# Prompt attention: the second key head's probabilities are scaled inside their transposition

## Chip, cores, metric

One Trainium2 chip, one core of it. The metric is the device time of one execution in microseconds, the median of several runs.

## What is computed

One inference step of a hybrid decoder layer for a prompt of 512 tokens and eight sample groups of four tokens, followed by a mixture of 32 experts. The change lies in the attention of the prompt. There, eight query heads share two key heads (four query heads each). Each query head has three branches, and each branch's result is weighted by a gate that was computed before:

```python
pr = masked_softmax(s + bias, mask)                       # per branch: exp(s - max) / sum
o_slc = einsum("bcgpkl,bcgkld->bcgpd", pr, kv[..., 1, :]) # selected blocks
o_win = einsum("bngpck,bnkgd->bncgpd", pr, kv[..., 1])    # sliding window
o_nsa = gn[0] * o_cmp + gn[1] * o_slc + gn[2] * o_win     # gates, one per token and head
```

With 512 tokens every causal block is selected and the window holds every earlier token, so both branches are causal attention over up to 512 keys.

## The kernel before

The program is a sequence of phases on all engines. Between two phases stands `phase_over()`, which clears the phase's semaphores and holds all engines at a barrier (line 214). The prompt attention is one phase; behind it come the branch gates with the output projection and the routing, and then the experts, which take more than half of the time.

The prompt attention works in **groups**, listed in `GROUPS_P` (lines 1521 to 1523): four groups for the cross-attention into memory (MEMB), one for each tile of 128 tokens, then for the tiles t = 3, 2, 1, 0 one group each of compressed (CMP), selected (SLC) and window (WIN) attention. A group of SLC or WIN has four **query steps**, one for each p in 0 to 3, and each step holds two query heads, one of either key head g; other groups have one step. That makes 40 query steps, 32 of them of SLC and WIN. Turning and multiplying with the values goes by **value steps**: t + 1 for a group of SLC or WIN (one for every 128 keys), one for the others, 28 in all, 20 of them of SLC and WIN.

Time is divided into **slots** (lines 1528 to 1532): slot s holds query step s. The value steps of a group begin three slots after its last query step (`LAG = 3`), one to a slot. Each engine runs its own list of this work in that order, and semaphores join them.

A query step of SLC or WIN, w = 128 (t + 1) keys wide, goes through the engines so:

- TensorE, `queries` (line 1764): one product of 64 x 128 by 64 x w for each g, into its own PSUM bank.
- VectorE, `scores_of` (line 1698): adds the position bias, writes to `probs` in SBUF and takes the maximum, one operation for each g.
- ScalarE, `exponentials` (line 1640): the exponential in place, with the sum of the row.
- VectorE, `scales` (lines 1720, 1721): reciprocal of the two sums, times the gates, into `scale_of`; this comes in VectorE's list between the next step's two scores, and waits until GpSimd is done with the step two before. The product with the gate raises `a_rc`.
- GpSimd (lines 1591 to 1595): waits for `a_rc`, multiplies the w columns of both heads by their factor in place, and raises `a_pr`.

A value step goes so:

- TensorE, `turn` (lines 1767 to 1784): waits until GpSimd has scaled the whole group, then transposes four heads of 128 x 128 for g = 0 into bank 4, and four for g = 1 into bank 5. Each half waits for the copy of the turn before out of its bank.
- ScalarE copies bank 4 (line 1599 through 1608) and VectorE bank 5 (line 1662) to `probT_p`.
- TensorE, `values` (line 1809): one slot later, two products of 128 x 64 by 128 x 512, accumulated over a tile's three branches in one bank.

TensorE's list for a slot is: turn, queries, and the values of the turn of the slot before. VectorE's is: copy of the turn, scores of g = 0, factors of the step before, scores of g = 1. `probs` has three buffers (`RING = 3`), used by groups in turn. A product in float32 shows as two records on TensorE, a transposition as one; each record has a weight load of its own.

SyncE loads the bias tables, the tokens and the first gate weights at the beginning of the phase (lines 1568 to 1576). Neither that nor any other transfer is touched.

Of the kernel before, what the change touches and what calls it, by code (L numbers as in the profile page):

```python
# [18 lines left out]
ALU = mybir.AluOpType  # L19
# [180 lines left out]
def build_program(nc, i, o, stop_after=99):  # L200

    ctx = ExitStack()
    with ctx:
        of_phase = []

        def sem(name):
            of_phase.append(nc.alloc_semaphore(name=name))
            return of_phase[-1]
# [33 lines left out]
        def bank(b, n=1):  # L242
            return psum[:, b] if n == 1 else psum[:, b:b + n]


        ident = take(128)
# [132 lines left out]
        src = lambda n: x[0:rows_of(n), n, :] if n < NT else mem[:, n - NT, :]  # L379
# [1126 lines left out]
        RING = 3  # L1506
        bias_q = take(8, NP_TOK)
        probs = take(RING, 8, 512)
        probT_p = take(2, 2, 512)
        peak = take(2, 8)  # L1510
        total = take(2, 8)
        scale_of = take(2, 8)
        assert cursor[0] <= w_gb_at
        cursor[0] = w_gb_at
        w_gb = take(6, KD, 128)
# [4 lines left out]
        SLC, WIN, CMP, MEMB = range(4)  # L1520
        GROUPS_P = [(MEMB, t) for t in range(TILES)]
# [34 lines left out]
        a_ex = sem("a_ex")  # L1556
        a_rc = sem("a_rc")
        a_pr = sem("a_pr")
        a_tp = sem("a_tp")
        a_ta, a_td = sem("a_ta"), sem("a_td")  # L1560
        a_pv = sem("a_pv")
# [3 lines left out]
        with nc.Block() as block:  # L1565
# [12 lines left out]
            @block.gpsimd  # L1578
            def _(pool):
                for i_q, (n, p) in enumerate(q_steps):  # L1580
                    kind, t = GROUPS_P[n]
                    c = scale_of[:, i_q % 2]
                    pool.wait_ge(a_rc, i_q + 1)
                    if kind == MEMB:
                        pool.tensor_tensor(mem_probs(n), mem_probs(n), c[:, 0:4].unsqueeze(2).to_broadcast([128, 4, MEM]),
                                           ALU.mult).then_inc(a_pr, 1)
                    elif kind == CMP:
                        pool.tensor_tensor(compact(n), compact(n), c.rearrange("q (g p) -> q g p", g=2).unsqueeze(3)
                                           .to_broadcast([128, 2, 4, NCMP_P]), ALU.mult).then_inc(a_pr, 1)
                    else:  # L1590
                        w = 128 * (t + 1)
                        for g in range(2):
                            rows = probs[:, n % RING, 4 * g + p, 0:w]
                            ins = pool.tensor_scalar(rows, rows, c[:, g:g + 1], None, ALU.mult)  # L1594
                        ins.then_inc(a_pr, 1)

            @block.scalar
            def _(act):
# [53 lines left out]
            def _(dve):  # L1652
# [49 lines left out]
                def scales(i_q):  # L1702

                    n, p = q_steps[i_q]
                    kind, t = GROUPS_P[n]
                    tot, c = total[:, i_q % 2], scale_of[:, i_q % 2]
                    gate = gates[:, t].rearrange("q (p g n) -> q n g p", p=4, g=2)
                    dve.wait_ge(a_ex, 2 * i_q + 2)
                    if i_q >= 2:
                        dve.wait_ge(a_pr, i_q - 1)  # L1710
                    if kind == MEMB:
                        dve.reciprocal(c[:, 0:4], tot[:, 0:4]).then_inc(a_rc, 1)
                    elif kind == CMP:
                        link(dve.tensor_reduce(tot.rearrange("q (g p) -> q g p", g=2), compact(n), AX, ALU.add))
                        link(dve.tensor_scalar(tot, tot, 1e-30, None, ALU.max))
                        link(dve.reciprocal(tot, tot))
                        dve.tensor_tensor(c.rearrange("q (g p) -> q g p", g=2), tot.rearrange("q (g p) -> q g p", g=2),
                                          gate[:, 0], ALU.mult).then_inc(a_rc, 1)
                    else:
                        link(dve.reciprocal(tot[:, 0:2], tot[:, 0:2]))  # L1720
                        dve.tensor_tensor(c[:, 0:2], tot[:, 0:2], gate[:, 1 + kind, :, p], ALU.mult).then_inc(a_rc, 1)  # L1721

                for slot in range(SLOTS_P):
                    if (j := turn_at(slot)) is not None:
# [9 lines left out]
            def _(pe):  # L1734
# [32 lines left out]
                def turn(j):  # L1767

                    n, a = v_steps[j]
                    kind, t = GROUPS_P[n]  # L1770
                    pe.wait_ge(a_pr, q_last[n] + 1)
                    for g in range(2):
                        if j:
                            pe.wait_ge((a_ta, a_td)[g], j)
                        for k in range(4):
                            if kind == MEMB:
                                src = mem_probs(n)[:, 2 * g + k // 2, 128 * (k % 2):128 * (k % 2) + 128]
                            elif kind == CMP:
                                src = compact(n)[:, g, k]
                            else:  # L1780
                                src = probs[:, n % RING, 4 * g + k, 128 * a:128 * a + 128]
                            rows = NCMP_P if kind == CMP else 128
                            mm = pe.transpose(bank(4 + g)[0:rows, 128 * k:128 * k + 128], src, ident)
                        mm.then_inc(a_tp, 1)

                def values(j):
# [729 lines left out]
```

## Time and profile before

| | |
|---|---|
| median of 3 runs | 2143.67 us (2143.18 to 2145.86) |
| the profiled execution | 2147.72 us |
| its span, first to last instruction | 2145.8 us |
| its mean granted TensorE clock | 0.946 |
| TensorE busy over the span | 1979.5 us, 92% |
| VectorE | 516.7 us, 24% |
| ScalarE | 407.5 us, 19% |
| GpSimd | 335.2 us, 16% |
| prompt attention | from about 527 to 645 us |

The busy time is a sum over phases with different limits. A group of instructions is named by its line in the kernel; a helper's line stands for all that call it. "Idle before" is the time the engine stood still directly before these instructions, with the engine and line that ended most of it. PE is TensorE's matrix work, PEld its weight loads, which run beside it; DVE is VectorE, ACT ScalarE, POOL GpSimd. PEclk is the granted share of TensorE's 2.4 GHz.

### The profile page before, as it was taken

The page shows a single profiled execution, that of the slowest core. Times are in us where ns is not written, and L with a number is a line of the kernel's source. Part 1 is how long each engine was busy: PE and PEld are TensorE (multiplying, and loading weights), DVE is VectorE, ACT ScalarE, POOL GpSimd, SP SyncE. Part 2 cuts the span into 40 slices and gives each one's busy share as a digit, 9 for nine tenths or more (in the row PEclk, how much of TensorE's full clock was granted, in tenths as well). Part 3 has the DMA queues.
Part 4 walks back from the last instruction along what each step waited for, and adds up shares of the span by engine and source line. Part 5 has one row for each costly group of instructions (what it writes and reads, how often), then busy time and mean ns, then how long its engine had stood idle before and what let it go on. Part 6 is the DMA issues. An engine that isn't in the chain of part 4 may idle for free.

```text
span 2145.8 us, 42699 instructions
## 1 busy us (share of the span) xinstructions
PE 1979.5 (92%) x17225; PEld 1038.0 (48%) x17225; DVE 516.7 (24%) x1342; ACT 407.5 (19%) x960; POOL 335.2 (16%) x359
## 2 busy tenths in 40 slices
PE   7997887788888999995999999999999999999995
PEld 3446773535447888644334444343443434444342
DVE  2224454241650111115211212112121211212111
ACT  3133561011650000000111111111111111111110
POOL 0010000000760000320112121121211112121121
PEclk9997987887999999996899999999999999999997
DMA  8116414231205110001999999999999999999994
GB/s 299 63 49 246 156 51 196 98 138 49 92 1 207 50 59 30 15 30 39 413 390 396 395 395 396 390 397 394 395 396 395 392 391 394 398 394 397 391 398 143
DMA packets 104369, 532.05 MB, mean 248 GB/s; under 512 B 15480, under 2 KB 32640, under 8 KB 52577
## 3 DMA queue, kind: packets, MB, share of 16 engines
q1 hardware_dynamic: 83721, 469.42, 55.4%
q0 software_dynamic: 19824, 59.12, 9.6%
q10 hardware_dynamic: 768, 2.75, 0.3%
q8 instruction: 36, 0.59, 0.1%
q14 instruction: 20, 0.16, 0.0%
HBM read 508.82 MB, written 28.91 MB: 251 GB/s over the span
## 4 chain that ended last, share of the span: by engine, by line
PE 49%; DMA 2%; ACT 1%; issue 0%; DVE 0%; POOL 0%; POOLq 0%; DVEq 0%
PE psum L2425 29%; PE psum L2438 16%; PE psum L2411 1%; PE psum L2474 1%; PE psum L2419 1%; DMA arena<-scr_h,arena 1%; PE psum L2464 1%; DMA y_sum<-arena 1%; ACT arena L2349 1%; POOL y_sum L2320 0%; ACT arena L2354 0%; DVE arena L2376 0%; PE psum L2455 0%; DVE arena L2372 0%; ACT arena L2335 0%
## 5 line engine op out<-in xcount | busy, mean ns | idle before, releaser
L2425 PE MATMUL psum<-arena 128*32 128x512 f32 x6144 | 666.9, 591 | 0.0
L2425 PEld LDWEIGHTS psum<-arena 128*32 128x32 f32 x6144 | 200.9, 108 | 447.3 <-issue 441.5
L2438 PE MATMUL psum<-arena 128*32 128x256 f32 x6144 | 344.8, 379 | 8.2 <-ACT arena L2349 8.2
L2438 PEld LDWEIGHTS psum<-arena 128*32 128x32 f32 x6144 | 191.3, 109 | 143.8 <-ACT arena L2349 15.7
L2390 DVE TENSOR_SCALAR arena<-psum 128x256 f32<-128x256 f32 x96 | 40.8, 425 | 883.0 <-PE psum L2425 880.3
L2320 POOL DMA_INDIRECT y_sum<-arena x96 | 149.3, 1555 | 620.1 <-ACT arena L2354 614.1
L2114 PE MATMUL psum<-arena 128*128 128x272 f32 x768 | 181.8, 394 | 1.4 <-PEq L217 1.4
L2114 PEld LDWEIGHTS psum<-arena 128*128 128x128 f32 x768 | 146.2, 191 | 34.8 <-issue 3.1
L2346 ACT ACTIVATE arena<-arena 128x256 f32<-128x256 f32 x96 | 40.1, 418 | 607.2 <-DVE arena L2390 607.2
L738 PE MATMUL psum<-arena 128*128 128x512 f32 (+3 forms) x320 | 112.5, 510 | 0.2 <-DVE arena L610 0.2
L2354 ACT ACTIVATE arena<-psum,arena 128x256 f32<-128x256 f32 x96 | 45.2, 471 | 187.4 <-PE psum L2438 187.4
L738 PEld LDWEIGHTS psum<-arena 128*128 128x128 f32 (+1 forms) x320 | 50.1, 175 | 62.9 <-issue 62.6
L949 DVE COPY arena<-psum 64x256 f32<-64x256 f32 (+1 forms) x144 | 57.6, 400 | 65.0 <-PE psum L1042 61.1
L2134 PE MATMUL psum<-arena 128*128 128x512 f32 (+1 forms) x160 | 71.1, 604 | 2.2 <-DVE arena L1975 2.2
L1594 POOL TENSOR_SCALAR arena<-arena 128x512 f32<-128x512 f32 (+3 forms) x64 | 68.4, 1082 | 23.8 <-DVE arena L1721 23.7
L1971 DVE TENSOR_TENSOR arena<-psum,arena 128x544 f32<-128x544 f32 x24 | 17.4, 724 | 218.8 <-ACT arena L1949 218.8
L1051 PE MATMUL psum<-arena 128*128 128x256 f32 (+1 forms) x288 | 68.0, 399 | 0.0
L2121 PE MATMUL psum<-arena 128*128 128x272 f32 x256 | 64.2, 399 | 4.1 <-DMA arena<-in_w_up 4.1
L1051 PEld LDWEIGHTS psum<-arena 128*128 128x128 f32 x288 | 57.2, 216 | 8.8 <-ACT arena L960 1.9
L2300 POOL COPY arena<-arena 96x1 uint32 (+1 forms) x33 | 6.1, 184 | 354.1 <-DMA y_sum<-arena 245.7
L1042 PE MATMUL psum<-arena 128*128 128x128 f32 (+1 forms) x288 | 43.1, 316 | 16.8 <-DVE arena L949 15.9
L1949 ACT ACTIVATE arena<-psum 128x544 f32<-128x544 f32 x24 | 15.0, 624 | 227.1 <-PE psum L2121 227.1
(353 smaller groups left out, 1755.2 us busy)
## 6 DMA issues: line engine op xcount, KB each, us to landing
arena<-in_w_gu SPq DMA_DIRECT2D x256, 1024.0 KB, 20.1
arena<-in_w_down SPq DMA_DIRECT2D x128, 1024.0 KB, 16.9
arena<-in_w_gb SPq DMA_DIRECT2D x24, 512.0 KB, 3.5
arena<-in_w_tok SPq DMA_DIRECT2D x3, 2048.0 KB, 10.3
arena<-in_x_all SPq DMA_DIRECT2D x8, 512.0 KB, 5.9
arena<-in_cache_mem SPq DMA_DIRECT2D x8, 512.0 KB, 3.6
arena<-in_cache_win SPq DMA_DIRECT2D x8, 512.0 KB, 4.1
arena<-in_w_up SPq DMA_DIRECT2D x1, 4096.0 KB, 13.4
```

Of the source, the lines that this page charges most:

```text
L738: mm = pe.matmul(bank(2 + c)[0:r, 0:b - a], dstT(n)[:, k], w_tok[:, k, a:b], start=(k == 0), stop=(k == KD - 1))
L949: copy(kvT[64 * a:64 * a + 64, c, 2 * q:2 * q + 2, g, 0:n], b[64 * g:64 * g + 64, :, a]).then_inc(s_kv, 1)
L1042: mm = pe.transpose(bank(q)[:, t * n:(t + 1) * n], rows[:, 4 * q + t, c], ident[0:n, 0:n])
L1051: mm = pe.matmul(bank(4 + c)[:, 0:2 * n].rearrange("p (g n) -> p g n", g=2), w_cmp[:, c, j], kvT[:, c, j, :, 0:n], start=(j == 0), stop=(j ...
L1594: ins = pool.tensor_scalar(rows, rows, c[:, g:g + 1], None, ALU.mult)
L2114: pe.matmul(bank(4 * s + h)[:, 0:HALF], w_gb[:, u % 6, k], hT[:, k, t], start=(k == 0), stop=(k == KD - 1))
L2121: mm = pe.matmul(bank(4 * s + 2 + h)[:, 0:HALF], w_up[:, k, 128 * c:128 * c + 128], oT_of(k)[:, t], start=(k == k0), stop=(k == k1 - 1))
L2134: mm = pe.matmul(bank(2 * (n % 2) + h)[0:r], mixT[:, k, 128 * n:128 * n + r], w_out[:, k, 512 * h:512 * h + 512], start=(k == 0), stop=(k ...
L2320: pool.indirect_dma_start(y_quarters, bass.IndirectOffsetOnAxis(cur_row[:, g:g + 1], 0), y_rows[:, g], None, compute_op=ALU.add).then_inc( ...
L2354: act.activation(y_rows[:, g], dn_half(g), ACT.Copy, scale=cur_gate[:, g:g + 1]).then_inc(e_yc, 1)
L2425: mm = pe.matmul(gu_bank(g)[32 * j:32 * j + 32].rearrange("p (h n) -> p h n", h=2), xgT[:, k, 32 * g:32 * g + 32], w_in_e[:, k, :, 256 * j ...
L2438: mm = pe.matmul(dn_half(g)[32 * j:32 * j + 32], actT[:, g, k % 2, 32 * (k // 2):32 * (k // 2) + 32], w_down_e[:, k, 256 * j:256 * j + 256 ...
```

## The change

The second key head's probabilities are no longer scaled on GpSimd. VectorE writes a 128 x 128 diagonal matrix with the factor (gate over sum) of the second head of each step, and the transposition of these probabilities becomes a float32 product with that diagonal, which turns and scales at once. The diagonals have a ring of three by four buffers beside `probs`. VectorE waits for the factor that it just made before it uses it; a turn of SLC or WIN waits for the diagonals of the group besides GpSimd's scaling. MEMB and CMP groups stay as they were.

```diff
@@ -1510,6 +1510,7 @@
         scale_of = take(2, 8)
+        diag = take(RING, 4, 128)
@@ -1556,6 +1557,7 @@
+        a_dg = sem("a_dg")
@@ -1589,10 +1591,8 @@
                         w = 128 * (t + 1)
-                        for g in range(2):
-                            rows = probs[:, n % RING, 4 * g + p, 0:w]
-                            ins = pool.tensor_scalar(rows, rows, c[:, g:g + 1], None, ALU.mult)
-                        ins.then_inc(a_pr, 1)
+                        rows = probs[:, n % RING, p, 0:w]
+                        pool.tensor_scalar(rows, rows, c[:, 0:1], None, ALU.mult).then_inc(a_pr, 1)
@@ -1719,6 +1719,8 @@
                         link(dve.reciprocal(tot[:, 0:2], tot[:, 0:2]))
                         dve.tensor_tensor(c[:, 0:2], tot[:, 0:2], gate[:, 1 + kind, :, p], ALU.mult).then_inc(a_rc, 1)
+                        dve.wait_ge(a_rc, i_q + 1)
+                        dve.tensor_scalar(diag[:, n % RING, p], ident, c[:, 1:2], None, ALU.mult).then_inc(a_dg, 1)
@@ -1769,6 +1771,8 @@
                     pe.wait_ge(a_pr, q_last[n] + 1)
+                    if kind in (SLC, WIN):
+                        pe.wait_ge(a_dg, sum(1 for m, p in q_steps[:q_last[n] + 1] if GROUPS_P[m][0] in (SLC, WIN)))
@@ -1780,7 +1784,11 @@
                             rows = NCMP_P if kind == CMP else 128
-                            mm = pe.transpose(bank(4 + g)[0:rows, 128 * k:128 * k + 128], src, ident)
+                            out = bank(4 + g)[0:rows, 128 * k:128 * k + 128]
+                            if g and kind in (SLC, WIN):
+                                mm = pe.matmul(out, src, diag[:, n % RING, k], start=True, stop=True)
+                            else:
+                                mm = pe.transpose(out, src, ident)
                         mm.then_inc(a_tp, 1)
```

## Rows read from the trace of the kernel before

**Rows 1.** Busy time by stage; columns: stretch, its length, each engine busy, clock, DMA

```profile
527.00:645.00 118.00, 98.06 (x608) 53.68 (x608) 72.78 (x264) 67.57 (x200) 78.29 (x72) 0.90 0.18 64
645.00:1015.00 370.00, 337.32 (x1378) 247.88 (x1378) 69.34 (x163) 27.14 (x46) 29.89 (x14) 0.93 0.18 59
```

**Rows 2.** Waits, 532 to 648 us: total, times, longest

```profile
PE psum L1783 <- POOL arena L1594: 15.2, 7, 5.3
```

**Rows 3.** Groups by shape, GpSimd, same stretch: busy, mean ns, idle before

```profile
L1594 POOL TENSOR_SCALAR arena<-arena 128x512 f32<-128x512 f32 x16 | 24.7, 1559 | 3.7 <-DVE arena L1721 3.7
...
L1594 POOL TENSOR_SCALAR arena<-arena 128x384 f32<-128x384 f32 x16 | 19.7, 1244 | 6.6 <-DVE arena L1721 6.6
...
L1594 POOL TENSOR_SCALAR arena<-arena 128x256 f32<-128x256 f32 x16 | 14.5, 923 | 5.9 <-DVE arena L1721 5.9
...
L1594 POOL TENSOR_SCALAR arena<-arena 128x128 f32<-128x128 f32 x16 | 9.5, 603 | 7.5 <-DVE arena L1721 7.5
```

**Rows 4.** Timeline, TensorE, 553 to 576 us: start, length, what, idle before

```profile
553.39 2.27 PE L1764 MATMUL psum<-arena 64*128 64x512 f32 x8
560.94 1.97 PE L1783 MATMUL psum<-arena 128*128 128x128 f32 x8 [5.28 <-POOL arena L1594]
...
575.23 1.09 PE L1783 MATMUL psum<-arena 128*128 128x128 f32 x8 [1.43 <-POOL arena L1594]
```

**Rows 5.** Timeline, TensorE, 578 to 645 us

```profile
578.11 1.09 PE L1783 MATMUL psum<-arena 128*128 128x128 f32 x8
579.13 0.92 PE L1764 MATMUL psum<-arena 64*128 64x384 f32 x4
579.98 1.08 PE L1809 MATMUL psum<-arena 128*64 128x512 f32 x4
...
602.14 1.09 PE L1783 MATMUL psum<-arena 128*128 128x128 f32 x8 [2.04 <-POOL arena L1594]
...
623.12 1.97 PE L1783 MATMUL psum<-arena 128*128 128x128 f32 x8 [2.62 <-POOL arena L1594]
...
634.64 1.09 PE L1783 MATMUL psum<-arena 128*128 128x128 f32 x8 [0.65 <-POOL arena L1594]
...
640.63 1.09 PE L1783 MATMUL psum<-arena 128*128 128x128 f32 x8 [2.94 <-POOL arena L1594]
```

**Rows 6.** Busy time and clock of short stretches; columns as in rows 1

```profile
561.00:564.00 3.00, 3.00 (x12) 2.02 (x12) 0.69 (x1) 0.60 (x1) 2.97 (x2) 0.50 0.00 0
...
600.00:602.00 2.00, 0.10 (x2) 0.00 (x0) 1.19 (x6) 1.18 (x4) 2.00 (x2) 1.00 0.00 0
...
623.00:629.00 6.00, 5.88 (x26) 4.45 (x28) 2.56 (x12) 2.56 (x9) 1.81 (x4) 0.50 0.00 0
```

**Rows 7.** Timeline, GpSimd, 545 to 578 us

```profile
548.53 15.44 POOL L1594 TENSOR_SCALAR arena<-arena 128x512 f32<-128x512 f32 x10 [1.83 <-DVE arena L1721]
565.79 9.38 POOL L1594 TENSOR_SCALAR arena<-arena 128x512 f32<-128x512 f32 x6 [1.83 <-DVE arena L1721]
```

**Rows 8.** Timeline, VectorE, 553 to 575 us

```profile
555.57 0.16 DVE L1721 TENSOR_TENSOR arena<-arena 128x2 f32<-128x2 f32 x1
...
557.91 0.17 DVE L1720 RECIPROCAL arena<-arena 128x2 f32<-128x2 f32 x1 [0.92 <-POOL arena L1594]
558.11 0.38 DVE L1721 TENSOR_TENSOR arena<-arena 128x2 f32<-128x2 f32 x1
...
571.29 0.42 DVE L1689 TENSOR_TENSOR arena<-arena 128x248 f32<-128x248 f32 x1
...
573.88 0.44 DVE L1715 TENSOR_SCALAR arena<-arena 128x8 f32<-128x8 f32 x1
```

**Rows 9.** Timeline, TensorE, 230 and 337 us: float32 products on the full array

```profile
230.08 2.75 PE L1051 MATMUL psum<-arena 128*128 128x256 f32 x12
...
337.67 0.38 PE L1366 MATMUL psum<-arena 128*128 128x127 f32 x2
337.88 0.31 PE L1367 MATMUL psum<-arena 128*128 128x32 f32 x2
```

**Rows 10.** Groups by shape, VectorE, whole span

```profile
L2084 DVE TENSOR_SCALAR arena<-arena 128x220 f32<-128x220 f32 x4 | 1.3, 330 | 0.0
```

## The prediction

> **What bounds the kernel now.** I read the views from the outside in. First the engine table by stage: the prompt attention runs from about 527 to 645 us, and the gate and routing stage behind it starts when the last engine of this one has finished [rows 1]. Between the two stands a barrier over all engines, and the only loads for later are issued at its start, so a microsecond won or lost in these 118 us is one in the end time. In the stage TensorE is busy 98.1 us and GpSimd 78.3 us. Neither share says who waits, so next comes the list of waits of the stretch: TensorE's matmuls in the turns (line 1783) stood still 15.2 us behind GpSimd's scaling (line 1594) [rows 2]. That is the most this change can take away directly. Third come GpSimd's four widths: 1.56, 1.24, 0.92 and 0.60 us for 512, 384, 256 and 128 columns, 16 of each, two per step [rows 3].
>
> Then the timeline of TensorE, to see where the 15.2 us lie. They are 5.28 us before 560.94, 1.43 before 575.23 [rows 4], 2.04 before 602.14, 2.62 before 623.12, 0.65 before 634.64 and 2.94 before 640.63 [rows 5]; what is left of the 15.2 is one short wait of 0.2. Between them, from 576 to 598 us and in most of the rest, TensorE is itself the bound: a turn takes 1.02 us to the start of the queries, those 0.85, the value products follow, and nothing stands still [rows 5]. So the change helps TensorE in a few gaps and makes it longer in the stretches between them.
>
> **Removed: 32 scalings on GpSimd**, one of each step's two. Their busy time is half of 68.4 us, or 34.2 us [rows 3], but only what a gap waits for comes back.
> - Gap at 560.94. GpSimd worked without a break from 548.53, ten operations of 1.54 us [rows 6]; the eighth, the end of the fourth step, releases the turn. VectorE had this step's factor ready at 555.57 [rows 7]. With one operation a step GpSimd has no queue there: 555.7 + 0.1 + 1.56 = 557.4. Gain 3.55 us.
> - Gap at 575.23: 1.43 us. One operation less (1.56) covers all of it. Gain 1.43.
> - Gaps at 602.14, 623.12, 634.64, 640.63. In each, GpSimd starts the last step's pair as soon as the factor is there, so one operation of that width goes: 1.24, 0.92, 0.60, 0.60 [rows 3]. The short wait of 0.2 goes too.
> Together 8.5 us. What is late next in these gaps is the chain scores, exponentials, factor; it remains.
>
> **Added on TensorE: 80 products in place of 80 transposes** (20 turns of the selected and window groups, four heads of the second key head). A transpose is one record, and eight come in a turn of 1.09 us, the last lasting 0.27: 0.117 us from start to start [rows 5]. The trace of before has no 128-column product on a full array in this stage. The nearest is line 1366, 127 columns: two records, and the next product starts 0.21 us later [rows 8]. Above it stands line 1051, 256 columns, 12 records in 2.75 us, 0.215 each, or 0.43 us a product [rows 8]. Below, a product could cost no more than the transpose; I see no reason for a gain. I take the nearest, 0.21: about 0.10 us more for each, 80 x 0.10 = 8.0 us, all of it where TensorE is the bound or right behind a gap. Ends: 0 and 80 x 0.32 = 25.6 us.
> The Trainium skill's page TensorE: Matmul & The Clock Gate (Terms, the entry on xbus) says that the transpose mode is four times as fast for FP32. By that rule each product would cost 0.47 us and the sum 28 us; the row of line 1366 says twice, not four times, and the measurement decides.
>
> **Added on VectorE: 32 diagonals**, each behind a wait for the factor made just before. A tensor_scalar of 220 columns takes 0.33 us [rows 9], the factor itself, 2 columns, 0.16 [rows 7]; between them by columns a 128-column one takes 0.26. The wait adds the space between two dependent operations. The reciprocal before a factor shows it: 557.91 to 558.11, 0.20 for an operation of 0.17 [rows 7]. Scores that used to start 0.11 after the factor (555.57) start about 0.3 us later. Queued behind the diagonal are the step's second scores, then ScalarE's exponential. In full slots this is covered: VectorE has some 2.4 us of work (two scores of 0.69, factor pair 0.33, copy 0.69) in a slot of 2.9 to 3.1. The cover is missing in the gaps, where the chain is what TensorE waits for. I count two diagonals before 557, one each before the gaps at 602, 623 and 634, three before the last: 8 x 0.3 = 2.4 us lost. Ends: 0 and, under GpSimd's hand, much more (a rival, below).
> The **new wait of a turn** on the diagonals costs nothing: the diagonal of a step is ready about 0.5 us after the factor starts, and GpSimd, released by the same factor, takes 0.60 at least plus the release. If that cover were gone, it would be 0.1 us for each of eight groups. The copy of the second bank on VectorE comes 0.4 us later after each turn. The values that read it are a slot away, so nothing. The added buffer and semaphore issue nothing. No transfer is moved.
>
> **The clock.** After 5.28 us without work TensorE runs at 0.50 of its 2.4 GHz (the 1.2 GHz level) for the whole of 561 to 564, and after 2.62 us from 623 to 629; after 2.04 us it stays at 1.00 [rows 10]. A stretch at half speed gives back half its length: 1.5 us and 3.0 us. The first gap becomes 5.28 - 3.55 + 0.6 = 2.3 us, between the two cases, so I take half, 0.75 us. The other becomes 2.62 - 0.92 + 0.3 = 2.0 us, which kept the clock elsewhere: 3.0 us.
>
> **Sum**: -8.5 + 8.0 + 2.4 - 3.75 = -1.85 us, rounded to -1.9. The profiled execution took 2147.7 us around its span of 2145.8; it would come to 2145.8. The median of the runs shown is 4 us lower, 2143.67, so 2141.8. A measurement of this kernel can tell about 0.2%, 4.3 us, from no change. So this is no change that can be seen.
> For the bounds: with no clock back and 0.12 us a product the sum is -8.5 + 9.6 + 3.2 = +4.3; with all the clock back, 0.09 a product and the diagonals half hidden it is -8.5 + 7.2 + 1.2 - 4.5 = -4.6. The forecast's own span is 2139 to 2148.
>
> **Rivals.**
> *Slower, GpSimd holds VectorE.* The factor that releases GpSimd's scaling stands right before the diagonal. If a VectorE operation on SBUF alone has to wait until the running GpSimd operation ends, each diagonal costs one scaling more. VectorE's slot becomes 2.4 + 0.3 + 1.56 = 4.3 us at 512 columns against 3.1 now, 2.1 + 0.3 + 1.24 = 3.6 against 2.9 at 384, about 0.4 more at 256: 8 x 1.2 + 8 x 0.7 + 8 x 0.4 = 18 us, so 2162. The point from which it decides is about 1 us a diagonal. For it: some short VectorE operations stretched beside GpSimd, 0.44 us for an 8-column one at 573.88. Against: GpSimd was busy from 565.79 to 575.17 in pieces of 1.56 [rows 6], none ended where that one did, and a 248-column operation with two SBUF inputs took its usual 0.42 at 571.29 [rows 7]. Chance 0.10.
> The Trainium skill's SBUF — State Buffer (Who interferes with whom) has this rule: the two share a port pair, held for a whole instruction, and the other is fully blocked. The two rows speak against it as written.
> *Slower, the product is four transposes.* +25.6 instead of +8.0: +15.7 us, 2159. Only line 1051, at twice the columns, is that dear. Chance 0.04.
> *Faster, the product hides.* If the second record of a product runs beside the next weight load, 80 x 0 instead of 8.0: -9.9 us, 2134. For it: value products with 64 weight columns and 512 moved take the same 1.08 us for four records as eight transposes (579.98) [rows 5], so forms differ. Against: line 1366. Chance 0.06.
> *The change doesn't do what it says*: GpSimd's queue may not be what the gap at 560.94 waits for, if the exponentials are late instead. Then 3.5 us less gain, +1.6, still no change; it belongs to the forecast.
>
> **How the numbers follow.** Forecast 0.80, of which 0.06 falls under -4.3 us and 0.07 over +4.3. Faster: 0.06 + 0.06 = 0.12. Slower: 0.10 + 0.04 + 0.07 = 0.21. Same: 0.67. The range 2138 to 2149.5 takes the forecast's span and a little of both sides; it leaves out the three rivals, 0.20.
>
> **What would show it.** GpSimd's line 1594 with 32 operations at the same four widths, and the waits of the turns on it down from 15.2 to some 7 us. In the turn from 576 to 598 us, 12 records in place of 8, and 1.4 us to the queries. VectorE's new line 32 times at about 0.26 us; at 0.8 or more beside GpSimd the first rival is true. The gap before the first selected turn shorter than 2.6 us. The clock at 1.00 near 623. The forecast is wrong if the stage is not between 111 and 123 us long.

## The result, and the profile after

The changed kernel took 2151.68 us in the median of 8 runs (2147.09 to 2153.26). The kernel before took 2145.7 us in the median of 8 (2141.12 to 2148.55; the three runs shown above are among them). The ratio is 1.0026, with a 95% interval of 1.0014 to 1.0038: slower by 6.0 us, or by 3.0 to 8.2 with the interval. Two further series of the same changed code, below, gave ratios of 1.0018 and 1.0011, so the loss is real and about 4 us. The forecast was 2141.8 us, no change, and its range of 2138.0 to 2149.5 does not hold the time. Of the 9.9 us between forecast and time, 2.0 lie in the starting point: the forecast started from 2143.67 us, the median of three runs, and eight gave 2145.7. Moved up by that, the range would end at 2151.5 and still not hold the time. Two single executions of more than 6000 us, one among the six of the product alone and one of the kernel before, are in no ratio.

One note for reading the prediction. From its sixth group on, it counts the rows differently from the section of rows ahead of it. Its [rows 6] is group 7 there (GpSimd's timeline), its [rows 7] is group 8 (VectorE's), its [rows 8] is group 9 (the products), its [rows 9] is group 10 (line 2084), and its [rows 10] is group 6 (the clock). From here on, groups have the numbers of that section.

The head of the page after, with busy time and count of each engine:

```profile
span 2146.7 us, 42859 instructions
PE 1983.7 (92%) x17305; PEld 1044.3 (49%) x17305; DVE 525.8 (24%) x1374; ACT 406.9 (19%) x960; POOL 304.4 (14%) x327
```

TensorE has 80 records more than before, which are the second records of 80 products. VectorE has 32 operations more and GpSimd 32 fewer. The change did what it says. The profiled execution took 2148.52 us.

The waits of the attention after, in all, times, longest:

```profile
POOL arena L1595 <- DVE arena L1721: 50.7, 32, 3.3
...
PE psum L1791 <- POOL arena L1595: 7.8, 5, 3.0
```

TensorE's wait on GpSimd fell from 15.2 us [rows 2] to 7.8, as forecast ("some 7 us"). GpSimd now waits 32 times for the factor, once in each step: it has no queue left.

Groups by shape after (count, busy us, mean ns):

```profile
L1789 PE MATMUL psum<-arena 128*128 128x128 f32 x160 | 22.8, 289 | 0.0
...
L1595 POOL TENSOR_SCALAR arena<-arena 128x512 f32<-128x512 f32 x8 | 13.3, 1657 | 10.4 <-DVE arena L1721 10.4
...
L1723 DVE TENSOR_SCALAR arena<-arena 128x128 f32<-128x128 f32 x32 | 9.2, 289 | 1.1
```

A diagonal takes 289 ns, against a forecast of 260. GpSimd's 512-column scaling takes 1657 ns, against 1559 [rows 3].

TensorE's timeline after: the first gap, one turn in the stretch where TensorE is the bound, and the last two long gaps:

```profile
554.64 0.66 PE L1791 MATMUL psum<-arena 128*128 128x128 f32 x4 [1.86 <-POOL arena L1595]
...
577.78 0.66 PE L1791 MATMUL psum<-arena 128*128 128x128 f32 x4
578.27 1.06 PE L1789 MATMUL psum<-arena 128*128 128x128 f32 x8
579.26 0.92 PE L1766 MATMUL psum<-arena 64*128 64x384 f32 x4
...
618.92 0.98 PE L1791 MATMUL psum<-arena 128*128 128x128 f32 x4 [1.80 <-POOL arena L1595]
619.70 1.92 PE L1789 MATMUL psum<-arena 128*128 128x128 f32 x8
...
636.34 1.12 PE L1791 MATMUL psum<-arena 128*128 128x128 f32 x4 [3.00 <-POOL arena L1595]
```

The first gap is 1.86 us where it was 5.28 [rows 4]. A turn in the full stretch takes 578.27 - 577.78 = 0.49 us for the four transposes and 579.26 - 578.27 = 0.99 us for the four products, 1.48 to the queries where it was 1.02 [rows 5].

So the parts of the attention moved much as forecast. To see where the 4 us are, the span has to be cut at points that both kernels have: the first attention matmul, the first matmul behind the attention's barrier, the first expert product, and the end of the last one. Each length below is a difference of such times on TensorE's timeline.

| us, profiled executions | attention | gates and routing | experts | rest to the end |
|---|---|---|---|---|
| before | 118.57 | 389.98 | 1084.92 | 24.89 |
| before, second profile | 118.49 | 390.57 | 1084.32 | 25.61 |
| changed | 118.15 | 388.17 | 1087.56 | 28.41 |
| changed, second profile | 118.10 | 388.80 | 1086.86 | 29.39 |

What lies ahead of the attention took 522.6 to 528.9 us over all 13 profiles of this study, and 524.4 and 528.3 in two of the same changed code. It moves with the execution and not with the edit, so it is left out. The four stages behind it are steady, and they give, as means of two, -0.4 in the attention, -1.8 in the middle, +2.6 in the experts and +3.7 in the rest: +4.1 us, within the measured interval. The attention, which the whole prediction was about, moved least of the four.

The rest to the end is short enough to read line by line. First before, then changed: GpSimd's last scatter of expert results, and SyncE's stores of the output.

```profile
2122.23 1.54 POOL L2320 DMA_INDIRECT y_sum<-arena  x1 [1.90 <-ACT arena L2354]
...
2136.38 2.51 SPq L2292 DMA_DIRECT2D out_y_prompt<-y_sum  x4
```

```profile
2119.60 1.54 POOL L2328 DMA_INDIRECT y_sum<-arena  x1 [1.91 <-ACT arena L2362]
...
2137.36 2.50 SPq L2300 DMA_DIRECT2D out_y_prompt<-y_sum  x4
```

From one to the other it is 14.15 us before and 17.76 after: 3.6 us more, and no line of this code was touched. The last scatters themselves are not slower: the three of this stretch land after 3.8 us in both traces (median). Between the two GpSimd waits for the scatters to land, then goes through the iterations of its loop over 54 blocks that are not used (32 blocks are, 22 are skipped by a branch), and raises the semaphore for which SyncE's stores wait. It computes nothing there, so the page has no group for it.

### The profile page after: what moved, and what is told of

Its sections match the earlier page's. It is cut to its first block, busy times and chain, and to the rows that moved or that the text cites. A ratio compares the mean times of both kernels' runs of the same rounds, so it can differ in the third digit from the quotient of the medians.

```text
span 2146.7 us, 42859 instructions
## 1 busy us (share of the span) xinstructions
PE 1983.7 (92%) x17305; PEld 1044.3 (49%) x17305; DVE 525.8 (24%) x1374; ACT 406.9 (19%) x960; POOL 304.4 (14%) x327
## 4 chain that ended last, share of the span: by engine, by line
PE 48%; DMA 2%; ACT 1%; issue 1%; DVE 0%; POOL 0%; POOLq 0%; DVEq 0%
PE psum L2433 28%; PE psum L2446 16%; PE psum L2419 1%; DMA y_sum<-arena 1%; DMA arena<-scr_h,arena 1%; PE psum L2482 1%; PE psum L2427 1%; PE psum L2472 1%; ACT arena L2357 1%; ACT arena L2362 0%; POOL y_sum L2328 0%; DVE arena L2384 0%; PE psum L2463 0%; DVE arena L2380 0%; ACT arena L2343 0%
## 5 line engine op out<-in xcount | busy, mean ns | idle before, releaser
L2122 PEld LDWEIGHTS psum<-arena 128*128 128x128 f32 x768 | 146.8, 191 | 34.4 <-issue 2.3
L2357 ACT ACTIVATE arena<-psum 128x256 f32<-128x256 f32 x96 | 33.4, 382 | 129.7 <-PE psum L2427 126.0
## 6 DMA issues: line engine op xcount, KB each, us to landing
arena<-in_w_tok SPq DMA_DIRECT2D x3, 2048.0 KB, 10.3
```

The costliest lines, as they stand in the source:

```text
L2122: pe.matmul(bank(4 * s + h)[:, 0:HALF], w_gb[:, u % 6, k], hT[:, k, t], start=(k == 0), stop=(k == KD - 1))
L2357: act.activation(actT[:, g].rearrange("p a n -> p (a n)"), at_half(g), ACT.Copy).then_inc(e_ae, 1)
```

## Experiments

**Is it real, and what is each part worth?** My theory then: the loss is outside of the attention. The rival: it is a difference between executions.

The changed kernel again, with no edit.

> The changed kernel again, unchanged, timed beside the kernel before, for a second trace of it. The first trace had the prompt attention at 118.15 us from its first matmul to the next stage's, against 118.57 before, while the medians were 6 us apart. Theory A (the stage loses it): the attention varies between executions with the clock gate, and the first trace was a lucky one; this trace shows 121 to 125 us for the stage, and the ratio is again about 1.0026. Theory B (the loss lies elsewhere): the stage is again 118.2 within 0.5 us, the ratio is again 1.002 to 1.003, and the stages behind the attention or the end of the kernel are longer than before. Theory C (mere scatter of the executions): the stage is 118.2 and the ratio falls within 0.999 to 1.001.

Measured: ratio 1.0018 (1.0007 to 1.0029), median 2149.53 us, the stages as in the table, and 17.82 us from the last scatter to the stores.

The kernel before again, with no edit.

> The kernel before against itself, to see how far two equal programs come apart by this measurement and how far its stages differ between two traces. All theories: ratio 1.000 within 0.001. Theory A expects its attention stage to vary by 2 us or more from 118.57; B and C expect it within 0.5 us, and that the stages before and behind it vary by several us.

Measured: 1.0004 (0.9994 to 1.0014), median 2146.27 us, 14.13 us from scatter to stores. The loss is real, and its two places, the experts and the rest, come back in a second profile of each kernel.

The product alone, with the plain identity. GpSimd still scales both heads. (In the diffs from here on, `...` stands for code left out between two places.)

```diff
+                            out = bank(4 + g)[0:rows, 128 * k:128 * k + 128]
+                            if g and kind in (SLC, WIN):
+                                mm = pe.matmul(out, src, ident, start=True, stop=True)
+                            else:
+                                mm = pe.transpose(out, src, ident)
```

> The kernel before, with the second key head's transpositions of the selected and window groups made as float32 products with the identity; GpSimd still scales both heads, no diagonals. The prediction's term: 80 products at 0.10 us more, 8.0 us, less what the seven waits on GpSimd (15.2 us) absorb, since GpSimd's scaling runs on while the turns are longer: stage 118.6 + 5 to 8 = 124 to 127 us. If the product cost as much as four transposes, the stage would be 140 us or more. Theory B adds that the total moves by more than the stage does.

Measured: 1.0041 (1.0025 to 1.0058), median 2155.69 us. The attention took 128.01 us, +9.5. A turn of the full stretch, from its timeline:

```profile
584.07 0.66 PE L1787 MATMUL psum<-arena 128*128 128x128 f32 x4
584.56 1.06 PE L1785 MATMUL psum<-arena 128*128 128x128 f32 x8
585.55 0.92 PE L1764 MATMUL psum<-arena 64*128 64x384 f32 x4
```

It is 0.49 + 0.99 = 1.48 us, 0.46 more than before [rows 5], or 0.115 us for each of its four products; 80 of them make 9.2 us. Scatter to stores stayed at 14.19 us, and 80 records more on TensorE left the end alone. So TensorE's code is not what made the rest longer.

The diagonals alone: VectorE builds them and TensorE waits for them, but nobody reads them.

```diff
+        diag = take(RING, 4, 128)
...
+        a_dg = sem("a_dg")
...
+                        dve.wait_ge(a_rc, i_q + 1)
+                        dve.tensor_scalar(diag[:, n % RING, p], ident, c[:, 1:2], None, ALU.mult).then_inc(a_dg, 1)
...
+                    if kind in (SLC, WIN):
+                        pe.wait_ge(a_dg, sum(1 for m, p in q_steps[:q_last[n] + 1] if GROUPS_P[m][0] in (SLC, WIN)))
```

> The kernel before, with VectorE's 32 diagonals, their wait and TensorE's wait on them, which nothing reads; GpSimd scales both heads and all transpositions stay. The prediction's term: 2.4 us on the path with GpSimd's queue gone, less here, because GpSimd's queue still hides it: stage 118.6 + 0 to 2 us. If each diagonal stood behind GpSimd's scaling (the rival with the held port), VectorE's new line would take 0.9 us or more and the stage 125 us or more. Theory B expects the total to move by 2 us or more although the stage does not.

Measured: 1.0011 (0.9997 to 1.0024), median 2147.29 us; the attention 119.05 us, +0.5; scatter to stores 14.18. This run also decides the rival in which GpSimd holds VectorE, because GpSimd is here without a break, as before. Its row, and three operations of VectorE beside it:

```profile
544.43 15.53 POOL L1596 TENSOR_SCALAR arena<-arena 128x512 f32<-128x512 f32 x10 [1.82 <-DVE arena L1723]
```

```profile
551.88 0.16 DVE L1723 TENSOR_TENSOR arena<-arena 128x2 f32<-128x2 f32 x1
552.08 0.29 DVE L1725 TENSOR_SCALAR arena<-arena 128x128 f32<-128x128 f32 x1
552.28 0.68 DVE L1700 CUSTOM_DVE_ANT_0 arena<-psum,arena 128x512 f32<-128x512 f32 x1
```

The diagonal starts 0.20 us after the factor, takes 0.29, and the scores start 0.20 behind it, with GpSimd in the middle of its ten. Nothing waits for GpSimd's operation to end. The four widths' means show what the overlap costs the other side: 1576, 1290, 961 and 649 ns here, against 1559, 1244, 923 and 603 before [rows 3]. With one diagonal to two scalings that is 0.02 to 0.05 us each.

The chain of a diagonal also shows in the waits of the attention: 16.0 us on GpSimd against 15.2, 1.3 on ScalarE's copy against 1.0, and one of 0.4 for a score that was late. That is 1.5 us. The stage grew only by 0.5, since the clock gave some back. Twelve microseconds behind the gap near 623, in the kernel before and in this one (the last but two of the columns is the clock):

```profile
623.12:635.12 12.00, 11.35 (x60) 7.00 (x61) 5.95 (x33) 6.89 (x25) 5.55 (x10) 0.76 0.00 1
```

```profile
619.82:631.82 12.00, 11.20 (x70) 6.75 (x72) 7.44 (x39) 7.58 (x27) 6.90 (x11) 0.86 0.00 1
```

A clock of 0.76 over 12 us loses 2.9 us, one of 0.86 loses 1.7: 1.2 us came back, although the gap ahead had grown from 2.62 to 2.70 us.

**What makes the rest longer?** Of the three parts, the one not yet run alone was the missing work on GpSimd. My theory was now that the loop which GpSimd runs empty takes longer when its code sits elsewhere. The rival was that the time has to do with when things arrive there.

Half of the scaling left out. This kernel leaves out the scaling of the second key head in the selected and window groups, and is otherwise the kernel before. Its first output is wrong by that, but 32 expert blocks ran as before, so its stages can be compared.

```diff
-                        for g in range(2):
-                            rows = probs[:, n % RING, 4 * g + p, 0:w]
-                            ins = pool.tensor_scalar(rows, rows, c[:, g:g + 1], None, ALU.mult)
-                        ins.then_inc(a_pr, 1)
+                        rows = probs[:, n % RING, p, 0:w]
+                        pool.tensor_scalar(rows, rows, c[:, 0:1], None, ALU.mult).then_inc(a_pr, 1)
```

> The kernel before with GpSimd scaling only the first key head of the selected and window groups, nothing in its place: the second head's scaling is left out. The prediction's terms for this part: 8.5 us of waits and up to 4.5 us of clock, so a stage of 105.5 to 110 us against 118.5. Theory B1 also expects 17.8 us from the last scatter to the first store, since GpSimd has 32 instructions less, as in the changed kernel; theory B2 expects 14.15. The output differs, so the routing may too, and with it the number of expert blocks; then the total says nothing and the stages are read.

Measured: 0.9983 (0.9972 to 0.9994), median 2140.98 us. The attention took 108.22 us, -10.3, but scatter to stores 17.71 us, and the whole gained 5 us only. The waits and one shape's row:

```profile
PE psum L1781 <- POOL arena L1593: 6.8, 4, 2.4
```

```profile
L1593 POOL TENSOR_SCALAR arena<-arena 128x512 f32<-128x512 f32 x8 | 12.5, 1568 | 9.4 <-DVE arena L1719 9.4
```

The waits fell by 8.4 us; the rest of the 10.3 is mostly the clock, which stayed up behind a first gap that was now 1.93 us (9.7 us lost to the clock in the stage, against 11.4). At 1568 ns the scaling is as fast as in the kernel before; in the changed kernel, with a diagonal beside each one, it is 0.09 us slower (1657). And this is the part that brings the longer end: nothing else was edited here.

The changed kernel with 32 empty instructions, and the kernel before with 16, on GpSimd behind the loop of the attention:

```diff
+                for _ in range(32):
+                    pool.nop()
```

> The changed kernel with 32 empty instructions on GpSimd behind its last scaling of the prompt attention, so that its later code lies where it lay before the change. GpSimd is idle there, so they cost nothing on the path. In both traces of the changed kernel the stretch from GpSimd's last scatter to the first store of the output was 17.8 us, in the three with GpSimd's code as before 14.15. Theory B1 (the position of GpSimd's later code costs it): this stretch is 14.2 us again, the attention stays at 118.1, and the ratio falls from 1.0018 to 1.000 to 1.001. Theory B2 (it is something else, as the new semaphore or VectorE's or TensorE's code): the stretch stays at 17.8.

> The kernel before with 16 empty instructions on GpSimd behind its last scaling of the prompt attention; nothing else. Theory B1: the attention stays at 118.5 us, and the stretch from the last scatter to the first store may take another value than 14.15, as 17.8, or stay, depending on where the loop then lies; any move of 1 us or more shows that position alone does it. Theory B2: it stays at 14.15 within 0.1.

Measured: 1.0011 (1.0000 to 1.0022), median 2147.59 us, for the first; 1.0 (0.9990 to 1.0010), 2144.26 us, for the second. Their pages begin

```profile
span 2151.2 us, 42859 instructions
```

```profile
span 2141.1 us, 42699 instructions
```

which are the counts of the two kernels without the additions. The empty instructions left nothing in the program, so neither run moved any code and neither tests the theory. They count as a third series and a third profile of each kernel: the attention took 118.16 and 118.56 us, scatter to stores 17.68 and 14.23, and the four stages together are 4.5 us longer in the changed kernel.

The product only where a gap is removed by it: groups 5, 12, 14 and 15, with 8 of the 20 turns. There GpSimd scales one head; elsewhere both, with transposes. The diff is against the changed kernel; TensorE's wait for the diagonals is limited to these groups in the same way. (Sixteen empty instructions were also meant to shift the code; they left nothing.)

```diff
+        BY_PRODUCT = (5, 12, 14, 15)
...
-                        rows = probs[:, n % RING, p, 0:w]
-                        pool.tensor_scalar(rows, rows, c[:, 0:1], None, ALU.mult).then_inc(a_pr, 1)
+                        for g in range(1 if n in BY_PRODUCT else 2):
+                            rows = probs[:, n % RING, 4 * g + p, 0:w]
+                            ins = pool.tensor_scalar(rows, rows, c[:, g:g + 1], None, ALU.mult)
+                        ins.then_inc(a_pr, 1)
...
+                        if n not in BY_PRODUCT:
+                            return
...
-                            if g and kind in (SLC, WIN):
+                            if g and n in BY_PRODUCT:
```

> The change only where TensorE waits for GpSimd: products with diagonals for four of the eight groups (selected of the last tile, window of the second tile, both of the first), GpSimd scales both heads of the other four, and 16 empty instructions keep GpSimd's later code in place. Eight products turns remain of 20. From the traces: four turns at 0.46 us, two, one and one, 3.7 us added; the gaps before the first selected turn, before the window turn of the second tile and in the first tile shorten by 3.4 us with 1.5 us of clock, by 0.9, and by 1.0. Theory of the stage: attention 112 to 116 us, total 2.5 to 6 us under the kernel before. If the gaps that are left grow as much as these shrink, the attention stays at 118.

Measured: 0.9995 (0.9983 to 1.0007), median 2145.63 us. The attention took 114.94 us, 3.6 less than before, and scatter to stores 17.65 us, 3.5 more: the gain is given back at the end. GpSimd has 16 operations fewer than before here, not 32, and the end is as late.

**Put the count back.** With real instructions this time, 32 memsets of one column at the head of GpSimd's part of the attention, where it waits for its first factor anyway.

```diff
+        spare = take(32)
...
+                for u in range(32):
+                    pool.memset(spare[:, u:u + 1], 0.0)
```

The changed kernel with them:

> The changed kernel with 32 one-column memsets on GpSimd at the head of the prompt attention, where it waits some 5 us for its first factor: real instructions in place of the 32 that the change took away (the empty ones of the two runs before leave no instruction in the program, so those kernels were copies of the changed one and of the one before). Theory B1 (position of GpSimd's later code): from last scatter to first store 14.2 us instead of 17.7, attention 118.1, ratio 1.000 to 1.001. Theory B2 (something else of GpSimd's stream, such as what its scaling line became): 17.7 us stays, ratio 1.001 to 1.003.

Measured: 0.9999 (0.9987 to 1.0011), median 2146.17 us. The attention took 118.16 us, as in the changed kernel. The end:

```profile
2116.72 1.54 POOL L2331 DMA_INDIRECT y_sum<-arena  x1 [1.90 <-ACT arena L2365]
...
2130.83 2.51 SPq L2303 DMA_DIRECT2D out_y_prompt<-y_sum  x4
```

That is 14.11 us. The 3.6 us are gone, for an addition of work.

The kernel before with them:

> The kernel before with the same 32 memsets: nothing of the change, only GpSimd's later code moved, by as many instructions to the other side. Theory B1: the stretch from last scatter to first store leaves 14.2 us, or keeps it if the positions that cost lie elsewhere; if it goes to 17 or 18 us, the total is 3 to 4 us over the kernel before though no work was added on any path. Theory B2: 14.2 us, total as before.

Measured: 1.0004 (0.9995 to 1.0013), median 2146.42 us; the attention 118.51 us, scatter to stores 14.19. So 32 instructions more than before do not lengthen the end, and the memsets themselves cost nothing that can be seen.

The product in groups 5 and 12 only, which removes 8 operations of GpSimd's, with 8 memsets in their place (the diff is against the four groups and the 32 memsets):

```diff
-        BY_PRODUCT = (5, 12, 14, 15)
+        BY_PRODUCT = (5, 12)
...
-                for u in range(32):
+                for u in range(8):
```

> Products with diagonals only for the two groups before whose turns TensorE waited longest for GpSimd's queue (selected of the last tile, window of the second), 6 of 20 turns, and 8 memsets in place of the 8 scalings that go. Against the version with four groups it leaves out the first tile, where the last gap stayed at 3.0 us with products. Stage theory: attention 114.9 less 0.5 to 1.5, so 113.4 to 114.5 us. Theory B1: from last scatter to first store 14.2 us; then the total is 4 to 5 us under the kernel before, ratio 0.998. Theory B2: 17.7 us and a ratio of 0.9995.

Measured: 0.9976 (0.9966 to 0.9985), median 2141.12 us, faster than both kernels. The attention took 114.90 us and scatter to stores 14.11. Its gaps, from the timeline:

```profile
555.12 0.66 PE L1799 MATMUL psum<-arena 128*128 128x128 f32 x4 [1.87 <-POOL arena L1600]
...
616.28 1.12 PE L1799 MATMUL psum<-arena 128*128 128x128 f32 x4 [1.81 <-POOL arena L1600]
...
633.57 1.97 PE L1799 MATMUL psum<-arena 128*128 128x128 f32 x8 [2.95 <-POOL arena L1600]
```

The two gaps where the product works are as short as in the changed kernel (1.87 and 1.81 against 1.86 and 1.80). The last is as before (2.95 against 2.94 [rows 5]). Only 6 turns, 24 products, pay: TensorE has 24 records more than before (17249 against 17225). No kernel with these 8 operations gone and nothing in their place was run, so this run shows a gain and not what 8 fewer would cost.

All profiled executions, by what GpSimd has more or fewer than the kernel before:

| GpSimd's operations against before | kernels | last scatter to stores, us |
|---|---|---|
| -32 | changed (three profiles), half of the scaling | 17.76, 17.82, 17.68; 17.71 |
| -16 | product in four groups | 17.65 |
| 0 | before (three profiles), product alone, diagonals alone | 14.15, 14.13, 14.23; 14.19; 14.18 |
| 0 | changed with 32 memsets, two groups with 8 | 14.11; 14.11 |
| +32 | before with 32 memsets | 14.19 |

## Why the prediction was wrong

The step that failed stands in its first paragraph: "a microsecond won or lost in these 118 us is one in the end time". That takes for granted that nothing else moves, a term put at nothing. The attention moved by -0.4 us, and the other stages by +4.5. The stage of 118.15 us met the prediction's own last sign, 111 to 123, which looked only at the stage.

The terms, with what the stage showed. The clock's term is 1 minus the clock, times the length, read in pieces of 4 us over the stage: 11.4 us lost before, 8.1 after.

| term | forecast | measured | from |
|---|---|---|---|
| TensorE's waits on GpSimd | -8.5 | -8.4 | half of the scaling left out: 15.2 to 6.8 |
| products | +8.0 | +9.2 | 80 x 0.115, product alone |
| diagonals | +2.4 | +1.5 | waits of the diagonals alone |
| clock | -3.75 | -3.3 | 11.4 to 8.1 |
| sum | -1.9 | -1.0 | |
| the stage | | -0.4 | 118.57 to 118.15 |

- **GpSimd.** Right: the first gap was to lose 3.55 us and shrank by 3.42.
- **The product.** Two records, as taken from line 1366 [rows 9]; 0.115 us more than a transpose and not 0.10. Neither other case came. It does not hide, and it is not four transposes. The measured price of a product of 128 columns is 0.99 / 4 = 0.25 us against 0.49 / 4 = 0.12. By the entry on xbus of the Trainium skill's page TensorE: Matmul & The Clock Gate (Terms) it should be four times, 0.49 us; the trace says twice.
- **The diagonal.** 289 ns against 260; its chain cost a little less than counted. As the prediction had it, its wait for TensorE costs nothing: the waits of the turns name GpSimd.
- **GpSimd holds VectorE.** False. A diagonal takes the same 0.29 us beside a GpSimd that never stops. The Trainium skill's page SBUF — State Buffer (Who interferes with whom) has it that one of the two is fully blocked while the other holds the port pair; it names for this the VectorE instructions in a two-port mode, which it allows a tensor_scalar, and those with two SBUF inputs beside a GpSimd that reads SBUF. The trace does not show this block. If such a hold takes place here, it costs GpSimd 0.09 us beside a diagonal and VectorE nothing.
- **The clock.** The size was about right, by luck: the places were not, and two errors cancel. The first gap gave back all, not half (no row of the first turns is stretched after it). The gap near 619 kept the clock less than thought: at 1.80 us, shorter than the 2.0 forecast, the turn behind it ran at the low level all the same. In the window of 12 us from 618.92 the clock was 0.86, a loss of 1.7 us where 2.9 were lost before, so 1.2 came back and not 3.0. In the changed kernel, columns as in rows 1:

```profile
619.00:622.00 3.00, 3.00 (x16) 2.78 (x16) 0.90 (x5) 0.98 (x3) 0.60 (x1) 0.52 0.00 0
622.00:630.00 8.00, 7.78 (x53) 4.25 (x52) 5.95 (x33) 5.23 (x19) 2.78 (x4) 0.97 0.01 3
```

Two smaller things in the recorded text. The price of the rival in which GpSimd holds VectorE, 2162 us, is 18 us on top of 2143.67 without the forecast's own -1.9; with it, 2160. And the terms measured here add up to -1.0 where the stage moved by -0.4; 0.6 us stays unexplained.

**What the +4.5 us outside are.** They are the longer end, two pieces of the experts' +2.6 us (2.3 together; the other 0.3 is spread over later blocks), and the shorter middle. The table has the last three for every kernel, in us: the middle stage (gates and routing), the first two expert blocks, each from its first product to the next block's, and the median time from GpSimd's last scatter of a block to its first operation for the next one.

| kernel | products | diagonals | GpSimd's operations | middle | first block | second block | scatter to next |
|---|---|---|---|---|---|---|---|
| before (three profiles) | 0 | 0 | 0 | 389.5 to 390.6 | 34.8 to 35.4 | 33.9 to 34.0 | 9.38 to 9.45 |
| before with 32 memsets | 0 | 0 | +32 | 390.3 | 35.0 | 33.8 | 9.40 |
| product alone | 80 | 0 | 0 | 388.3 | 34.7 | 34.0 | 9.42 |
| diagonals alone | 0 | 32 | 0 | 390.3 | 36.4 | 33.9 | 9.36 |
| half of the scaling | 0 | 0 | -32 | 390.4 | 34.9 | 34.4 | 9.59 |
| four groups | 32 | 16 | -16 | 388.6 | 35.9 | 34.0 | 9.54 |
| two groups with 8 memsets | 24 | 8 | 0 | 389.3 | 35.6 | 33.9 | 9.47 |
| changed with 32 memsets | 80 | 32 | 0 | 388.7 | 36.1 | 33.9 | 9.41 |
| changed (three profiles) | 80 | 32 | -32 | 388.2 to 388.8 | 35.9 to 36.3 | 34.9 to 35.1 | 9.62 to 9.71 |

*The longer end, 3.6 us,* goes with fewer instructions on GpSimd ahead of its skipped iterations. That is shown: it came with 16 and with 32 fewer, in five profiles of five, and it went from the changed kernel when 32 others stood in their place. It is not only at the end. In the used blocks too, each pass of GpSimd's loop takes 0.1 to 0.3 us longer in the kernels with fewer (9.54 to 9.71 against 9.36 to 9.47). Before, then changed, between the last two blocks:

```profile
2088.38 1.54 POOL L2320 DMA_INDIRECT y_sum<-arena  x1 [1.90 <-ACT arena L2354]
2097.83 0.18 POOL L2300 COPY arena<-arena 96x1 uint32 x1 [7.91 <-DMA y_sum<-arena]
```

```profile
2085.76 1.54 POOL L2328 DMA_INDIRECT y_sum<-arena  x1 [1.91 <-ACT arena L2362]
2095.39 0.18 POOL L2308 COPY arena<-arena 96x1 uint32 x1 [8.09 <-issue]
```

That is 9.45 and 9.63 us. The 3.6 us spread over 22 skipped iterations would be 0.16 each, the same size; this is an estimate. Why a pass is longer is open. The number of instructions also sets at what address the loop's code lies, and no run varied one without the other.

*The second block, 1.2 us,* is a consequence of the same loop. GpSimd's pass behind the first block took 10.7 to 10.8 us in the three profiles of the changed code, 10.6 with half of the scaling and 10.4 with the four groups, against 9.8 to 10.2 in all kernels with as many operations as before or more. With its next pass GpSimd gathers the rows of a later block's tokens. They then land too late, and TensorE waits for them:

```profile
1067.83 1.54 POOL L2328 DMA_INDIRECT y_sum<-arena  x1 [1.84 <-ACT arena L2362]
1078.67 0.18 POOL L2308 COPY arena<-arena 96x1 uint32 x1 [9.31 <-issue]
1079.74 0.97 POOL L2311 DMA_INDIRECT arena<-scr_h,arena  x1 [0.88 <-POOL arena L2308]
```

```profile
1088.92 0.88 PE L2419 MATMUL psum<-arena 96*128 96x96 f32 x8 [1.14 <-DMA arena<-scr_h,arena]
```

This wait is 1.14, 1.20 and 0.97 us in the changed kernel and 0.47 with half of the scaling, and no other kernel has it in this block. So the four groups, whose pass is the least late, have the longer end and not this loss.

*The first block, 1.1 us,* goes with the diagonals: 35.6 to 36.4 us in the seven profiles that have them, the diagonals alone among them, and 34.7 to 35.4 in the six that have none. The granted clock over its first 22 us was 0.88 to 0.92 with them and 0.93 to 0.96 without; it reached the full level later. Why, some 400 us behind the last diagonal, stays open.

*The middle, -1.8 us,* goes with the products: 388.2 to 389.3 us in the seven profiles with products, the product alone among them, and 389.5 to 390.6 in the six without. So it does not come from GpSimd, and its cause stays open too. The clock in the routing's products near the end of this stage is not it. Over the same ten microseconds of work it was low or high in either kernel. Before, twice, then changed, twice (the clock is again the last but two of the columns):

```profile
998.85:1008.85 10.00, 8.31 (x46) 7.51 (x46) 7.18 (x22) 0.00 (x0) 0.00 (x0) 0.67 0.00 0
```

```profile
996.60:1006.60 10.00, 7.46 (x46) 6.38 (x46) 7.72 (x24) 0.00 (x0) 0.00 (x0) 0.80 0.00 0
```

```profile
994.89:1004.89 10.00, 7.19 (x46) 6.16 (x46) 7.72 (x24) 0.00 (x0) 0.00 (x0) 0.84 0.00 0
```

```profile
995.31:1005.31 10.00, 8.34 (x46) 7.38 (x46) 7.42 (x23) 0.00 (x0) 0.00 (x0) 0.67 0.00 0
```

## What to carry to other kernels

A part that wins in a few gaps and costs in every turn should be used for the gaps alone: here 24 products in place of 80 kept 3.7 us of a gain that the other 56 had eaten. Cut the whole span at fixed marks before explaining a small difference, since here all of the loss lay in stages that the edit does not touch. Put a stage's lengths from all kernels beside what each of them has of the change: that sorts the pieces by cause, and it shows what only moves with the execution. Where such a stage is a loop that an engine runs empty, change the number of that engine's instructions ahead of it and look again before blaming the edit, and make sure that what is added is in the program.

## What the runs showed that I had not expected

- From GpSimd's last scatter, over its landing and 22 skipped iterations, to the stores behind them it takes 14.1 to 14.2 us or 17.7 to 17.8 us, with nothing in between in 13 profiles, by how many instructions GpSimd has ahead of them.
- How long TensorE was idle did not decide whether its clock fell. The turn behind the pause ran at the low level after 1.80, 1.81, 2.37, 2.62 and 3.00 us, and at the high one after 1.72, 1.86, 1.87, 1.93, 2.04 and, with the diagonals alone, 2.70 and 3.58 us. At the last gap of the stage, with the same eight transposes behind it, the turn took 1.09 us behind 2.94 in the kernel before [rows 5] and 1.97 behind 2.95 with two groups. What else decides, no run was made for. So a price for the clock read from the length of a gap alone is good to a microsecond or two.
- An f32 tensor_scalar of 128 columns on VectorE, 289 ns here, ran at full pace beside GpSimd, and only GpSimd's operation became 0.09 us longer.
